# Second mixer of a three-layer kernel: logarithm and exponential for the roots, squares and splits on other engines, rotation and key norms earlier

## The chip, the core and the metric

The kernel runs on one core of a Trainium2 chip. A core has four compute engines that run their own instruction streams and meet through semaphores: TensorE (PE, matrix products; its weight loads are listed as PEld), VectorE (DVE), ScalarE (ACT) and GpSimd (POOL); SyncE (SP) issues most transfers. They share one on-chip memory, SBUF; the products land in eight banks of a second one, PSUM. The metric is the device time of one execution in microseconds (us); lower is better.

## The reference

Three transformer layers run one after the other on 256 tokens (and 256 context tokens) of width 1024, all in float32. The part that matters here is the mixer of the second layer, latent attention with 8 heads. `h` and `hc` are the normalised, modulated tokens and context tokens:

```python
c_q, c_kv, k_pe = split(h @ w_down, [384, 640])      # "down"; widths 384, 256, 64
q = (rmsnorm(c_q, q_lora_norm) @ w_uq)               # "up": 8 heads x (128 + 64), tokens only
kv = (rmsnorm(c_kv, kv_lora_norm) @ w_ukv)           # 8 heads x (128 key + 128 value), tokens and context
q = split_norm(q, q_norm)                            # rmsnorm of the 128 and of the 64 apart
k_nope = rmsnorm(k_nope, k_norm[:128]); k_pe = rmsnorm(k_pe, k_norm[128:])
q[..., 128:], k_pe = rope(q[..., 128:]), rope(k_pe)  # the tokens' own alone
p = softmax(q @ [k_nope, k_pe].T * 192 ** -0.5);  o = p @ v;  x = x + g1 * (o @ w_out)

def rmsnorm(x, g): return x * rsqrt(mean(x * x) + 1e-6) * g
```

## The kernel before

**Weights.** Every weight is streamed once, in slots of 128 x 1024 float32, through a ring of 8 raw buffers that SyncE fills. A product keeps float32 precision by splitting both operands in two: ScalarE copies the raw slot to a rounded `whi` (L369, `hi_slot`, ring of 4), GpSimd subtracts to get `wlo = raw - whi` (L374, `lo_slot`), and TensorE adds the products hi x hi, hi x lo and lo x hi (`slot_products`, L387). The activations are split in the same way. GpSimd does nothing else in this part of the program. The queues are in order on every engine; the order of the work is written out by hand, one function for each engine: `mla_pe`, `mla_act`, `mla_dve`.

**The mixer, on TensorE.** Tokens lie along the columns, features along the partitions. Six "down" tiles come first (`MLA_SRC`): 0 to 2 are the query latents `cq` (256 columns), 3 and 4 the key latents `ckv` (512), 5 the key's rotated part `kpe` (512). Tiles 0 to 3 run paced by the layer's norm; tiles 4 and 5 are whole `column_tile`s. The sum of squares of a latent is a product with a matrix of ones (`down_sums(g)`, L1479; g = 0 query latents, 1 key latents, 2 `kpe`). `mod_turn` transposes a row of the modulation. Then 14 "up" steps follow (`UP`): s = 0 to 5 are two query heads' worth each, 6 to 9 keys, 10 to 13 values. Behind step s = j + 1 stands the sum of the squares of query group j (L1544), which waits for `m_qsq`, the squares themselves; since the queue is in order, step s + 1 stands behind that wait. Behind steps 8 to 11 stand the keys' sums (L1554). Behind step 12 stand three products with a permutation (L1563) that swap the halves for the rotation. `keep_running(pe, 7, 4)` (L460) is four products whose result nobody reads. Products of the modulation (L514) follow, then the scores of the first pair of heads (L1573, L1576).

**On ScalarE.** It evicts each tile from PSUM (L1464 down, L1664 query, L1670 key, L1673 value), squares (L1652 latents, L1668 query), makes `whi`, and takes the roots: for latents a square root (`std`, L627), for queries and keys a logarithm behind each sum (L632) and later, for all together, an exponential (L636, `inverse_root`). When the function set that is loaded lacks the next function, the compiler puts an `ACT_TABLE_LOAD` ahead of it; `preload_act_table_set(LN_EXP)` loads a set with both logarithm and exponential.

**On VectorE.** For latents it takes the reciprocal of the root (L1733), scales (L1738), rounds to the hi part (L1743) and subtracts for the lo part (L1744), which signals `m_clo`; the first up step waits for three of these. Then it squares the keys (L1755), scales the queries (L1748), rotates query and key (L1776 to L1781), and scales the keys (L1760), before the maxima of the scores (L1790).

Of the kernel before, what the change touches and what calls it, by code (L numbers as in the profile page):

```python
# [161 lines left out]
def build(nc, wstream, params, consts, x_in, ctx_in, mem_in, pos_in, w2_in, gla_c, mla_c, sec_c, out):  # L162
    with ExitStack() as ctx:
# [1310 lines left out]
        def mla_pe(pe):  # L1474
# [6 lines left out]
            for m, (name, j, ntok) in enumerate(MLA_SRC):  # L1481
# [16 lines left out]
                elif m >= 4:  # L1498
                    column_tile(pe, START["cq"] + m, DOWN_BANK[m], xhi, xlo, ntok)
                    if m == 4:  # L1500
                        down_sums(0)
                        mod_turn(pe, 5)
            down_sums(1)
            for s, (n, half) in enumerate(UP):
                bank = 2 * (s % 2)
                if s == 0:
                    pe.wait_ge(S["m_clo"], 3)
                    pe.wait_ge(S["m_dn"], 6)
                elif s == 1:
# [26 lines left out]
                if 1 <= s <= 6:  # L1536
# [19 lines left out]
                if s == 12:  # L1556

                    pe.wait_ge(S["m_qn"], 6)
                    pe.wait_ge(S["m_cn"], 6)
                    pe.wait_ge(S["m_klog"], 4)  # L1560
                    pe.wait_ge(S["late_in"], 16)
                    for j, x in enumerate((mq[:, 8:10, :], mq[:, 10:12, :], kpe[:, T:TT])):
                        nc.tensor.matmul(ps[:, 4 + j, 0:T if j == 2 else TT], mlac[:, 0:P], x, start=True, stop=True).then_inc(S["m_sw"], 1)  # L1563
# [76 lines left out]
        def mla_act(act):  # L1640
            def down_std(g):
                m0, cnt, bank, n, ntok = MLA_NORM[g]
                act.wait_ge(S["m_css"], g + 1)
                std(mrst[:, g, 0:ntok], ps[:, bank, 0:ntok], n).then_inc(S["m_cstd"], 1)
            for m, (name, j, ntok) in enumerate(MLA_SRC):
# [7 lines left out]
                if m >= 1:  # L1653
# [3 lines left out]
                if m == 3:  # L1657
                    down_std(0)
            down_std(1)
            for s, (n, half) in enumerate(UP):  # L1660
                up_done(act, s)
                b = 2 * (s % 2)
                if s < 6:
                    nc.scalar.activation(mq[:, 2 * s:2 * s + 2, :], ps[:, b:b + 2, 0:T], ACT.Copy).then_inc(S["m_ev"], 1)  # L1664
                    if s in (0, 3):
                        act.wait_ge(S["m_css"], s // 3 * 2 + 1)
                    act.wait_ge(S["m_ev"], s + 1)
                    nc.scalar.activation(Hf1[:, s, :], mq[:, 2 * s:2 * s + 2, :], ACT.Square).then_inc(S["m_qsq"], 1)  # L1668
# [24 lines left out]
                if s == 11:  # L1693
                    act.wait_ge(S["m_klog"], 4)
                    for i in range(4):
                        inverse_root(Hf1[:, 2 * i:2 * i + 2, :]).then_inc(S["m_krstd"], 1)
# [30 lines left out]
        def mla_dve(dve):  # L1727
# [970 lines left out]
```

## Time and profile before

| | us |
|---|---|
| median of 3 runs | 1294.65 (1293.46 to 1294.67) |
| the profiled execution, whole | 1295.5 |
| its span, first to last instruction | 1293.3 |
| PE busy | 1260.4 (97%) |
| ACT busy | 716.6 (55%) |
| POOL busy | 715.4 (55%) |
| DVE busy | 587.7 (45%) |

The profile lists for each engine the time in which it was busy. The chain that ended last is, at each step, what released the instruction that stood there; in the table of the page 73% of it is PE. The trace lists each instruction with its start, counted from the start of the span. A releaser behind "idle before" is the instruction that ended a wait. Matmuls overlap, so the length of a group of them is some 0.2 us more than the distance to the next group; distances between starts are the safer number. The granted clock is the share of full speed that TensorE was given: 1.00 is 2.4 GHz, 0.5 is 1.2 GHz.

### The profile page before, as it was taken

Reading aid. Unit: us, or ns where it says so; the run is one execution under the profiler, and the core shown is the slowest. Engines: PE = TensorE matmul, PEld = TensorE weight load, DVE = VectorE, ACT = ScalarE, POOL = GpSimd, SP = SyncE. Lnnn points to the kernel's source line nnn. Section 1 sums busy time; section 2 is a strip of 40 time slices with the busy share of each in tenths; the row PEclk is TensorE's granted clock in tenths of the full one; section 3 lists DMA queues with packets and bytes.
Section 4 is the critical chain, followed back from the end, with each engine's and each line's share of the span. In section 5 each row is a group of like instructions: output and inputs, shape, how many; then the busy total and the mean of one; then the engine's idle time right before and its main releaser. Section 6 shows DMA issues by size and latency. Waiting matters only on the chain.

```text
span 1293.3 us, 21900 instructions
## 1 busy us (share of the span) xinstructions
PE 1260.4 (97%) x8008; PEld 1083.7 (84%) x8008; DVE 587.7 (45%) x1065; ACT 716.6 (55%) x1096; POOL 715.4 (55%) x335
## 2 busy tenths in 40 slices
PE   5999999999999999999998999999999999999999
PEld 1688678778888888888777658899999977999999
DVE  3424672237444444210166464555532585666610
ACT  3572356337544544421367554777775667877752
POOL 0442234253444444454445034688898874988897
PEclk8999999999999999999998999999999999999999
DMA  9533753742323333634523334566666540666663
GB/s 362 194 100 106 277 197 131 291 162 73 107 97 97 103 108 97 233 113 135 213 82 116 125 134 161 192 196 195 195 212 197 181 144 33 219 200 193 198 202 129
DMA packets 60132, 210.16 MB, mean 163 GB/s; under 512 B 6432, under 2 KB 9760, under 8 KB 59936
## 3 DMA queue, kind: packets, MB, share of 16 engines
q1 hardware_dynamic: 59632, 207.52, 47.9%
q10 hardware_dynamic: 432, 1.70, 0.3%
q8 instruction: 46, 0.75, 0.2%
q14 instruction: 22, 0.18, 0.0%
HBM read 208.15 MB, written 1.05 MB: 162 GB/s over the span
## 4 chain that ended last, share of the span: by engine, by line
PE 73%; POOL 12%; issue 6%; DVE 4%; ACT 2%; DMA 2%; SPq 0%; POOLq 0%; DVEq 0%; ACTq 0%
PE ps L387 56%; POOL wlo L374 12%; PE ps L514 2%; DMA raw<-wstream 2%; PE ps L1594 1%; PE ps L1573 1%; PE ps L1189 1%; PE ps L442 1%; PE ps L1177 1%; PE ps L424 1%; PE ps L434 1%; ACT whi L369 1%; PE ps L1157 1%; DVE Hlo_ L733 1%; DVE ps L747 1%
## 5 line engine op out<-in xcount | busy, mean ns | idle before, releaser
L374 POOL TENSOR_TENSOR wlo<-raw,whi 128x1024 fp32r<-128x1024 f32 x291 | 687.4, 2381 | 503.7 <-ACT whi L369 503.3
L369 ACT ACTIVATE whi<-raw 128x1024 fp32r<-128x1024 f32 x291 | 306.5, 1057 | 192.9 <-PE ps L387 132.9
L387 PE MATMUL ps<-Hhi_,whi 128*128 128x256 f32 (+1 forms) x1336 | 379.8, 314 | 0.1
L387 PE MATMUL ps<-Hlo_,whi 128*128 128x256 f32 (+1 forms) x1336 | 376.2, 311 | 0.0
L387 PEld LDWEIGHTS ps<-Hhi_,whi 128*128 128x128 f32 x1336 | 255.1, 191 | 16.6 <-issue 4.1
L387 PEld LDWEIGHTS ps<-Hlo_,whi 128*128 128x128 f32 x1336 | 255.1, 191 | 13.6 <-issue 1.4
L387 PE MATMUL ps<-Hhi_,wlo 128*128 128x256 f32 (+1 forms) x1336 | 224.8, 311 | 0.1
L387 PEld LDWEIGHTS ps<-Hhi_,wlo 128*128 128x128 f32 x1336 | 193.8, 191 | 12.7 <-POOL wlo L374 0.3
L387 PE MATMUL ps<-hidhi,whi 128*128 128x256 f32 (+1 forms) x528 | 148.3, 311 | 0.1
L387 PE MATMUL ps<-hidlo,whi 128*128 128x256 f32 (+1 forms) x528 | 147.8, 310 | 0.0
L814 ACT ACTIVATE u<-ps,par 128x256 f32<-128x256 f32 (+1 forms) x132 | 82.6, 626 | 82.5 <-PE ps L387 78.2
L865 DVE SCALAR_TENSOR_TENSOR u<-ps,par,u 128x255 f32<-128x255 f32 (+1 forms) x132 | 73.4, 556 | 81.9 <-ACT u L814 81.9
L387 PEld LDWEIGHTS ps<-hidhi,whi 128*128 128x128 f32 x528 | 100.8, 191 | 6.6 <-DVE XT L989 1.7
L387 PEld LDWEIGHTS ps<-hidlo,whi 128*128 128x128 f32 x528 | 100.8, 191 | 4.7
L989 DVE SCALAR_TENSOR_TENSOR XT<-ps,ada,XT 128x256 f32<-128x256 f32 x48 | 21.6, 479 | 156.1 <-PE ps L387 153.5
L387 PE MATMUL ps<-hidhi,wlo 128*128 128x256 f32 (+1 forms) x528 | 89.1, 310 | 0.0
L868 DVE SCALAR_TENSOR_TENSOR u<-ps,par,u 128x255 f32<-128x255 f32 (+1 forms) x132 | 75.5, 572 | 17.8 <-DVE u L865 0.5
L387 PEld LDWEIGHTS ps<-hidhi,wlo 128*128 128x128 f32 x528 | 76.4, 191 | 4.7
L823 ACT ACTIVATE hidhi<-ps 128x256 f32 (+3 forms) x66 | 52.0, 788 | 45.3 <-DVE ps L876 45.3
L882 DVE TENSOR_TENSOR hidlo<-ps,hidhi 128x256 f32 (+3 forms) x66 | 52.6, 797 | 51.2 <-ACT hidhi L823 51.2
L514 PE MATMUL ps<-raw,cs 128*32 128x512 f32 x304 | 45.4, 645 | 13.5 <-DMA raw<-wstream 13.4
L820 ACT ACTIVATE ps<-u 128x256 f32<-128x256 f32 (+1 forms) x66 | 30.3, 460 | 47.9 <-DVE u L868 47.5
(342 smaller groups left out, 1592.3 us busy)
## 6 DMA issues: line engine op xcount, KB each, us to landing
raw<-wstream SPq DMA_DIRECT2D x367, 512.0 KB, 3.5
Haside_lo<-wstream SPq DMA_DIRECT2D x8, 512.0 KB, 6.1
Haside_hi<-wstream SPq DMA_DIRECT2D x8, 512.0 KB, 9.2
Paside<-wstream SPq DMA_DIRECT2D x4, 512.0 KB, 4.7
XT<-x_t SPq DMA_DIRECT2D x1, 1024.0 KB, 10.6
XT<-ctx_t SPq DMA_DIRECT2D x1, 1024.0 KB, 12.6
memx<-mem_t ACTq DMA_DIRECT2D x1, 1024.0 KB, 5.5
out_t<-XT SPq DMA_DIRECT2D x1, 640.0 KB, 6.1
```

The source lines that it names most:

```text
L369: nc.scalar.activation(whi[:, n % RING, :], raw[:, r % RAWS, :], ACT.Copy).then_inc(S["hi_ready"], 1)
L374: nc.gpsimd.tensor_tensor(wlo[:, r, :], raw[:, r, :], whi[:, n % RING, :].bitcast(F32), ALU.subtract).then_inc(S["lo_ready"], 1)
L387: mm = nc.tensor.matmul(o, a, b, start=start, stop=stop)
L424: nc.tensor.matmul(ps[:, bank, 0:ntok], wlo[:, RAW_OF[n + s] % RAWS, k * P:(k + 1) * P], xhi(k), start=False, stop=False)
L514: mm = nc.tensor.matmul(ps[32 * g:32 * g + 32, MOD_BANK[batch], :], cs[:, k, 6 - 2 * v:38 - 2 * v], rows[:, 512 * (k % 2):512 * (k % 2) + ...
L814: nc.scalar.activation(acc[:, j % 4, :], ps[:, j % 4, 0:ntok], ACT.Identity, scale=pdyn(f"cw{f}_1", i * 8 + j), bias=pdyn(f"cb{f}", i * 8 ...
L820: nc.scalar.activation(ps[:, HID_BANK, 0:ntok], acc[:, (2 * q + 1) % 4, :], ACT.Silu).then_inc(S[f"{t}_s"], 1)
L823: nc.scalar.activation(hid_row(hi, ntok, q, i), in_turn(ps[:, HID_BANK, 0:ntok]), ACT.Copy).then_inc(S[f"{t}_hi"], 1)
L865: nc.vector.scalar_tensor_tensor(seg(acc, 1, T), seg(tile, 0, T - 1), pdyn(f"cw{f}_0", i * 8 + j), seg(acc, 1, T), ALU.mult, ALU.add).then ...
L868: nc.vector.scalar_tensor_tensor(seg(acc, 0, T - 1), seg(tile, 1, T), pdyn(f"cw{f}_2", i * 8 + j), seg(acc, 0, T - 1), ALU.mult, ALU.add). ...
L882: nc.vector.tensor_tensor(hid_row(lo, ntok, q, i), in_turn(hf), hid_row(hi, ntok, q, i).bitcast(F32), ALU.subtract).then_inc(S[f"{t}_pair" ...
L989: ins = nc.vector.scalar_tensor_tensor(x, y, ada[L][:, bass.ds(m * 2 + 16 * part_ + h, 1)], x, ALU.mult, ALU.add)
```

## The change

1. **Latents' roots.** `down_std` takes the logarithm and, right behind it, the exponential, in place of the square root; VectorE's reciprocals (L1733) go. The rounding of the three query latents to their hi part moves from VectorE to ScalarE (`m_chi`).
2. **Sums amid the fifth down tile.** TensorE does tile 4's hi products, then `down_sums(0)`, then tile 4's lo products. ScalarE makes the weight slot that it made behind the second square one square later.
3. **Queries.** The exponential stands behind each logarithm, one group at a time. The squares move from ScalarE (L1668) to VectorE (`query_squares`), where they stand among the splits of the key latents and the scalings of the queries.
4. **Keys.** The exponential stands behind each logarithm too, so the scalings `key_norm` can follow one by one; all four stand ahead of the first maxima.
5. **Rotation.** The permutation of `kpe` moves behind step 2, that of the queries behind step 7, and VectorE's rotations with them.
6. **Rest.** Up steps use the other pair of PSUM banks, `keep_running` goes, and `out_act("mo")` no longer loads the set LN_EXP.

```diff
@@ out_act
-            nc.scalar.preload_act_table_set(LN_EXP)
+            if stage != "mo":
+                nc.scalar.preload_act_table_set(LN_EXP)
@@ mla_pe
-                elif m >= 4:
+                elif m == 4:
+                    n = START["cq"] + m
...
+                    for o, c0, width, _, x, start, stop in his:
+                        nc.tensor.matmul(o, whi[:, n % RING, c0:c0 + width], x, start=start, stop=stop)
+                    down_sums(0)
+                    pe.wait_ge(S["lo_ready"], n + 1)
+                    for o, c0, width, _, x, start, stop in los:
+                        mm = nc.tensor.matmul(o, wlo[:, RAW_OF[n] % RAWS, c0:c0 + width], x, start=start, stop=stop)
+                    mm.then_inc(S["slot_used"], 1)
+                    mod_turn(pe, 5)
+                elif m == 5:
                     column_tile(pe, START["cq"] + m, DOWN_BANK[m], xhi, xlo, ntok)
-                    if m == 4:
-                        down_sums(0)
-                        mod_turn(pe, 5)
...
-                bank = 2 * (s % 2)
+                bank = 2 * ((s + 1) % 2)
...
+                    if j == 3:
+                        pe.wait_ge(S["m_rot"], 1)
...
+                if s == 2:
...
+                    nc.tensor.matmul(ps[:, 7, 0:T], mlac[:, 0:P], kpe[:, T:TT], start=True, stop=True).then_inc(S["m_sw"], 1)
+                if s == 7:
+                    pe.wait_ge(S["m_qn"], 6)
+                    for j, x in enumerate((mq[:, 8:10, :], mq[:, 10:12, :])):
+                        nc.tensor.matmul(ps[:, 6 + j, :], mlac[:, 0:P], x, start=True, stop=True).then_inc(S["m_sw"], 1)
...
-            keep_running(pe, 7, 4)
+            pe.wait_ge(S["m_klog"], 4)
@@ mla_act
-                std(mrst[:, g, 0:ntok], ps[:, bank, 0:ntok], n).then_inc(S["m_cstd"], 1)
+                alink(log_square(mrst[:, g, 0:ntok], ps[:, bank, 0:ntok], n))
+                inverse_root(mrst[:, g, 0:ntok]).then_inc(S["m_cstd"], 1)
...
+                    for k in range(3):
+                        act.wait_ge(S["m_cn"], k + 1)
+                        nc.scalar.activation(cqhi(k), in_turn(mla_dst(k)), ACT.Copy).then_inc(S["m_chi"], 1)
...
-                    nc.scalar.activation(Hf1[:, s, :], mq[:, 2 * s:2 * s + 2, :], ACT.Square).then_inc(S["m_qsq"], 1)
...
+                    act.wait_ge(S["m_qlog"], j + 1)
+                    inverse_root(query_root(j)).then_inc(S["m_qrstd"], 1)
@@ mla_dve
-                nc.vector.reciprocal(mrst[:, g, 0:ntok], mrst[:, g, 0:ntok]).then_inc(S["m_crv"], 1)
...
+            def query_squares(j):
...
+                x = mq[:, 2 * j:2 * j + 2, :]
+                nc.vector.tensor_tensor(Hf1[:, j, :].rearrange("p (a t) -> p a t", t=T), x, x, ALU.mult).then_inc(S["m_qsq"], 1)
...
+            for m in range(3):
+                latent_norm(m)
+            for m in range(3):
+                dve.wait_ge(S["m_chi"], m + 1)
+                nc.vector.tensor_tensor(cqlo(m), in_turn(mla_dst(m)), cqhi(m).bitcast(F32), ALU.subtract).then_inc(S["m_clo"], 1)
+            latent_norm(3)
+            key_split(3)
+            query_squares(0)
+            latent_norm(4)
+            key_split(4)
+            latent_norm(5)
+            query_squares(1)
+            query_squares(2)
...
+            for j in range(3, 6):
+                query_squares(j)
+                query_norm(j - 3)
```

The first place is TensorE's queue at the fifth down tile (L387 before, L1504 and L1508 after: its products; L1479, L1480: the sums of the query latents; L533: `mod_turn`). Before:

```order
L387 MATMUL ps<-Hhi_,whi 128x512
L387 MATMUL ps<-Hlo_,whi 128x512
L387 MATMUL ps<-Hhi_,wlo 128x512 [waits lo_ready]
L387 MATMUL ps<-Hhi_,wlo 128x512 x7
L1479 MATMUL ps<-Hf,con 128x256 [waits m_csq]
L1479 MATMUL ps<-Hf,con 128x256 x2
L533 MATMUL ps<-sel,modrow 128x8 [waits mod_row]
```

And now:

```order
L1504 MATMUL ps<-Hhi_,whi 128x512
L1504 MATMUL ps<-Hlo_,whi 128x512
L1480 MATMUL ps<-Hf,con 128x256 [waits m_csq]
L1480 MATMUL ps<-Hf,con 128x256 x2
L1508 MATMUL ps<-Hhi_,wlo 128x512 [waits lo_ready]
L1508 MATMUL ps<-Hhi_,wlo 128x512 x7
L533 MATMUL ps<-sel,modrow 128x8 [waits mod_row]
```

The three sums have moved ahead of the tile's eight lo products.

The second place is VectorE's queue behind the query latents' splits. Before (L1733 reciprocal, L1738 scaling, L1743 rounding, L1744 lo part, L1755 squares of the keys):

```order
L1733 RECIPROCAL mrq<-mrq 128x512 [waits m_cstd]
L1738 SCALAR_TENSOR_TENSOR ckv<-ckv,par,mrq 128x512 [waits m_crv]
L1743 CAST ckvhi<-ckv 128x256x2 [waits m_cn]
L1744 TENSOR_TENSOR ckvlo<-ckv,ckvhi 128x256x2 [waits dve_step]
L1738 SCALAR_TENSOR_TENSOR ckv<-ckv,par,mrq 128x512
...
L1738 SCALAR_TENSOR_TENSOR kpe<-kpe,par,mrq 128x512 [waits m_crv]
L1755 TENSOR_TENSOR Hf<-kn 128x1024 [waits m_qss,m_ev,m_cn]
```

Now (L1751 scaling, L1757 and L1758 the split, L1766 squares of the queries, L1771 their scaling):

```order
L1751 SCALAR_TENSOR_TENSOR ckv<-ckv,par,mrq 128x512 [waits m_cstd]
L1757 CAST ckvhi<-ckv 128x256x2 [waits m_cn]
L1758 TENSOR_TENSOR ckvlo<-ckv,ckvhi 128x256x2 [waits dve_step]
L1766 TENSOR_TENSOR Hf<-mq 128x512 [waits m_css,m_ev]
L1751 SCALAR_TENSOR_TENSOR ckv<-ckv,par,mrq 128x512 [waits m_cstd]
...
L1751 SCALAR_TENSOR_TENSOR kpe<-kpe,par,mrq 128x512 [waits m_cstd]
L1766 TENSOR_TENSOR Hf<-mq 128x512 [waits m_ev] x2
```

The reciprocals are gone, and the squares of the first query group stand right behind the split of the first key latent.

The third place is ScalarE's queue at the first two up steps (L1664 eviction, L1668 squares, L369 `whi`, L627 square root, L632 logarithm). Before:

```order
L1664 ACTIVATE mq<-ps 128x512 [waits slot_used]
L1668 ACTIVATE Hf<-mq 128x512 [waits m_ev]
L369 ACTIVATE whi<-raw 128x1024 [waits slot_used,raw_in0]
L632 ACT_TABLE_LOAD
L632 ACTIVATE mrq<-ps,con 128x512 [waits m_qss]
```

Now (L1684 eviction, L636 exponential):

```order
L1684 ACTIVATE mq<-ps 128x512 [waits slot_used]
L369 ACTIVATE whi<-raw 128x1024 [waits slot_used,raw_in0]
L632 ACTIVATE mrq<-ps,con 128x512 [waits m_qss]
L636 ACTIVATE mrq<-mrq 128x512 [waits m_qlog]
```

The squares and the load are gone, and the exponential is new. No `ACT_TABLE_LOAD` is left between the down projection and the end of the output projection.

## Rows read from the trace of the kernel before

**Rows 1.** TensorE's timeline, 655 to 745 us: start, length, line, [idle before].

```profile
678.05 1.88 PE L1479 MATMUL ps<-Hf,con 128*128 128x512 f32 x4
683.39 2.93 PE L387 MATMUL ps<-cqsplit,whi 128*128 128x256 f32 x12 [3.46 <-DVE cqsplit L1744]
```

**Rows 2.** The chain that ended last, 665 to 760 us: start, length, what.

```profile
683.39 4.21 PE ps L387 x18
687.60 1.71 PE ps L1479 x2
689.31 2.19 PE ps L387 x18
691.50 0.86 PE ps L1544 x2
692.37 2.01 PE ps L387 x18
...
734.43 1.73 PE ps L460 x8
```

**Rows 3.** Busy time by stretches; PEclk is the granted share of the clock.

```profile
core 0: us, PE busy (x) PEld busy (x) DVE busy (x) ACT busy (x) POOL busy (x), PEclk, DMA share, GB/s
...
683.40:691.34 7.94, 7.94 (x38) 6.91 (x39) 7.77 (x7) 2.75 (x4) 1.35 (x1) 0.61 0.22 66
...
739.66:794.60 54.94, 53.79 (x268) 34.46 (x265) 32.27 (x53) 25.86 (x55) 9.93 (x4) 1.00 0.32 120
```

**Rows 4.** VectorE's timeline, 655 to 745 us and 739 to 815 us.

```profile
673.08 0.50 DVE L1730 TENSOR_SCALAR gsc<-par 128x2 f32<-128x2 f32 x1
...
679.38 0.62 DVE L1744 TENSOR_TENSOR cqsplit<-cq,cqsplit 128x256 fp32r<-128x256 f32 x1
...
680.77 2.57 DVE L1744 TENSOR_TENSOR cqsplit<-cq,cqsplit 128x256 fp32r<-128x256 f32 x1
...
686.55 0.75 DVE L1738 SCALAR_TENSOR_TENSOR ckv<-ckv,par,mrq 128x512 f32<-128x512 f32 x1
687.33 0.64 DVE L1743 CAST ckvhi<-ckv 128x512 fp32r<-128x512 f32 x1
688.01 1.10 DVE L1744 TENSOR_TENSOR ckvlo<-ckv,ckvhi 128x512 fp32r<-128x512 f32 x1
...
707.58 1.88 DVE L1755 TENSOR_TENSOR Hf<-kn 128x1024 f32<-128x1024 f32 x1 [10.19 <-ACT kn L1670]
...
714.26 1.22 DVE L1755 TENSOR_TENSOR Hf<-kn 128x1024 f32<-128x1024 f32 x1
...
771.40 2.99 DVE L1799 TENSOR_SCALAR Pm<-Pm,arec 128x512 f32<-128x512 f32 x2
```

**Rows 5.** GpSimd's timeline, 640 to 830 us.

```profile
680.53 2.34 POOL L374 TENSOR_TENSOR wlo<-raw,whi 128x1024 fp32r<-128x1024 f32 x1 [3.34 <-ACT whi L369]
...
706.02 2.36 POOL L374 TENSOR_TENSOR wlo<-raw,whi 128x1024 fp32r<-128x1024 f32 x1 [0.30 <-ACT whi L369]
...
771.50 2.62 POOL L374 TENSOR_TENSOR wlo<-raw,whi 128x1024 fp32r<-128x1024 f32 x1 [1.58 <-ACT whi L369]
```

**Rows 6.** ScalarE's timeline, 655 to 745 us.

```profile
678.25 0.60 ACT L1464 ACTIVATE kpe<-ps 128x512 f32<-128x512 f32 x1 [3.50 <-PE ps L387]
...
679.42 1.04 ACT L369 ACTIVATE whi<-raw 128x1024 fp32r<-128x1024 f32 x1
680.36 0.67 ACT L627 ACTIVATE mrq<-ps,con 128x512 f32<-128x512 f32 x1
...
687.64 0.60 ACT L1664 ACTIVATE mq<-ps 128x512 f32<-128x512 f32 x1 [6.61 <-PE ps L387]
...
711.63 0.61 ACT L636 ACTIVATE cq<-cq 128x512 f32<-128x512 f32 x1
```

**Rows 7.** ScalarE's function-set loads in groups by line, 657 to 740 us.

```profile
L632 ACT ACT_TABLE_LOAD x2 | 2.6, 1283 | 0.0
L636 ACT ACT_TABLE_LOAD x2 | 2.6, 1283 | 0.0
...
L627 ACT ACT_TABLE_LOAD x1 | 1.3, 1283 | 0.0
```

**Rows 8.** DMA issues of weight slots, whole run: count, size, median us to landing.

```profile
raw<-wstream SPq DMA_DIRECT2D x367, 512.0 KB, 3.5
```

More of the change, by code:

```diff
@@ L1550, in mla_pe @@
                         pe.wait_ge(S["m_qlog"], 6)
+                    if i == 1:
+                        pe.wait_ge(S["m_rot"], 2)
                     if i >= 2:
@@ L1555, in mla_pe @@
                     mm.then_inc(S["m_kss"], 1)
[L1556 to L1563, printed above, removed]
             def scores(p, qt):
@@ L1692, in mla_act @@
                     log_square(Hf1[:, 2 * i:2 * i + 2, :], ps[:, 4 + 2 * (i % 2):6 + 2 * (i % 2), :], 128).then_inc(S["m_klog"], 1)
[L1693 to L1696, printed above, removed]
+                    act.wait_ge(S["m_klog"], i + 1)
+                    inverse_root(Hf1[:, 2 * i:2 * i + 2, :]).then_inc(S["m_krstd"], 1)
             def exps(p, qt):
@@ new lines, in mla_dve @@
+            latent_norm(5)
+            query_squares(1)
+            query_squares(2)
+            dve.wait_ge(S["m_sw"], 1)
+            dlink(nc.vector.tensor_tensor(Hf1[:, 7, 0:T], ps[:, 7, 0:T], sin, ALU.mult))
+            dve.wait_ge(S["m_cn"], 6)
+            dlink(nc.vector.tensor_tensor(kpe[:, T:TT], kpe[:, T:TT], cos, ALU.mult))
+            nc.vector.tensor_tensor(kpe[:, T:TT], kpe[:, T:TT], Hf1[:, 7, 0:T], ALU.add).then_inc(S["m_rot"], 1)
+            for j in range(3, 6):
+                query_squares(j)
+                query_norm(j - 3)
@@ L1761, in mla_dve @@
+            query_norm(3)
             key_squares(0)
-            dve.wait_ge(S["m_qrstd"], 1)
-            for j in range(3):
-                query_norm(j)
+            query_norm(4)
+            query_norm(5)
             key_squares(1)
-            for j in range(3, 6):
-                query_norm(j)
-            key_squares(2)
-            key_squares(3)
             dve.wait_ge(S["m_qn"], 6)
             dve.wait_ge(S["m_sw"], 3)
-            dve.wait_ge(S["late_in"], 16)
-            cos, sin = mlac[:, P:P + T], mlac[:, P + T:P + 2 * T]
@@ L1777, in mla_dve @@
             dlink(nc.vector.tensor_tensor(x, x, cos.rearrange("p (a t) -> p a t", a=1).to_broadcast([P, 4, T]), ALU.mult))
+            key_squares(2)
+            dve.wait_ge(S["m_rot"], 2)
             nc.vector.tensor_tensor(x, x, tmp, ALU.add).then_inc(S["m_rot"], 1)
-            dlink(nc.vector.tensor_tensor(mrst[:, 0, 0:T], ps[:, 6, 0:T], sin, ALU.mult))
-            dlink(nc.vector.tensor_tensor(kpe[:, T:TT], kpe[:, T:TT], cos, ALU.mult))
-            nc.vector.tensor_tensor(kpe[:, T:TT], kpe[:, T:TT], mrst[:, 0, 0:T], ALU.add).then_inc(S["m_rot"], 1)
@@ L1783, in mla_dve @@
             key_norm(0)
-            key_norm(1)
+            key_squares(3)
+            for i in range(1, 4):
+                key_norm(i)
             def maxes(p, qt):
```

58 lines of the change are left out of this document (29 added, 29 removed).

## The prediction

> **What bounds the kernel now.** I read the busy table first: PE is busy 97% of the span, so the change can only help by removing TensorE work, a TensorE wait, or time at the lower clock. The edits lie in the second mixer, so I read TensorE's timeline there. It has one long wait: the second latents' sums start at 678.05 and the first up step at 683.39, 3.46 us idle, released by VectorE's last lo part of the query latents [rows 1]. Behind it the granted clock of the next 7.94 us is 0.61, a mix of 1.2 and 2.4 GHz, though TensorE is busy throughout [rows 3]. In the chain that ended last the same work shows it: an up step of 18 products takes 4.21 and then 2.19 us, where the third takes 2.01; the sum between them takes 1.71, where a later one takes 0.86 [rows 2]. So one late split costs 3.46 us idle and (1 - 0.61) x 7.94 = 3.1 us of slow clock. Third, `keep_running` holds TensorE for 1.73 us [rows 2], 1.8 with its hand-over. From the first scores to the second output tile TensorE is busy 53.79 of 54.94 us [rows 3], so nothing that VectorE or ScalarE do sooner there is worth more than a microsecond.
>
> **Part 1 and 2, latents' roots and the sums amid tile 4.** The sums come ahead of eight lo products, and their root has no table load ahead of it. ScalarE can then have the inverse root by about 671.4. VectorE is held until its modulation bias and `gsc`, 673.08 + 0.50 [rows 4], since these stand ahead and wait for `mod_turn`, whose place on TensorE does not move. From 673.6 it has three scalings and three lo parts (0.5 and 0.6 us each, the latter [rows 4]), with ScalarE's rounding beside them: done at about 676.5 to 677, against 679.8 when TensorE wants them. The split is no longer late, by a margin of 3 us; even a GpSimd piece of 2.4 us in between keeps it. The 3.46 us and the 3.1 us go: **-6.6**. TensorE's own products stay the same in number. The reciprocals that go were hidden for keys and `kpe`, and the added exponentials (0.6 us each by the 512-column one, [rows 6]) lie on a ScalarE that waits for TensorE.
>
> **Part 6.** `keep_running` goes: -1.8. The four products of modulation unit 9 read raw slots, and the last of these is freed only when the last up step ends; a slot lands a median 3.5 us after its issue [rows 8], and TensorE now wants it some 3.1 us later (seven of the eight slots' products at 0.45 us). I take a wait of 0.2, between 0 and 0.6: **-1.6**.
>
> **Table loads.** Five of 1.28 us go inside the mixer [rows 7] and one more in the output projection. ScalarE waits for TensorE around them all, except that the first lay in the latents' root, counted above. Worth nothing more: 0.
>
> **Part 3, the squares on VectorE.** This is the step that decides. First what the rows show. A VectorE instruction with both inputs in SBUF waits when GpSimd is in a piece of `wlo`. The lo part that takes 0.62 us alone took 2.57 when it started at 680.77, with a GpSimd piece from 680.53 to 682.87; it ended 0.47 after the piece. The squares of the keys take 1.22 us alone, and 1.88 when started at 707.58 inside the piece of 706.02 to 708.38 [rows 4, 5]. And the port changes hands between two VectorE instructions when GpSimd asks: two scalings started at 771.40 took 2.99 together, because a piece asked at 771.50, waited 0.27 (2.62 for 2.35) and then ran between them [rows 4, 5]. Before the change the query squares were on ScalarE, which the rows never show waiting so.
>
> The Trainium skill states the same in "SBUF — State Buffer", section Who interferes with whom: a VectorE instruction with two SBUF inputs and a GpSimd instruction that reads SBUF exclude each other for the whole instruction, and whichever issued first keeps the port. The rows agree (2.57 for 0.62). By a reading of the edit without this rule the total below would be 7 us lower; it speaks against this part of the change.
>
> Now the schedule after. TensorE: sums end 679.8; step 0 2.0, the `kpe` sum 0.86, step 1 2.0 [rows 2]: at 684.7 it wants the squares of query group 0, which VectorE must have made. ScalarE: `kpe` is evicted at 678.25, the slot copy at 679.42 ends at 680.46 and the root at 680.36 moves behind it as now [rows 6], logarithm 0.67 and exponential 0.6: the keys' root is there at 681.6. GpSimd starts its piece at 680.53, as before [rows 5]. VectorE therefore asks for the first key latent's scaling at 681.65, inside the piece; it runs at 682.75 and ends at 683.5 (0.75). The rounding takes 0.64, to 684.2. By then ScalarE has evicted step 0 (681.8 + 0.2 drain, 0.60) and copied the next slot (1.04, to 683.5), so GpSimd is in its next piece, 683.6 to 685.95. The lo part of 1.10 us waits for it and ends at 686.9. During it the slot copy behind step 1's eviction ends (684.9 + 0.5 + 1.04 = 686.4), GpSimd asks and takes the port at 686.8, as at 771.50, to 689.1. The squares of group 0 are next on VectorE: they wait for this third piece and end at 689.7 (0.69 us, an estimate between half the 1.22 of the keys' squares and the 0.75 of a scaling of the same size). TensorE waits from 684.7 to 689.75: **+5.1**. Everything behind it on TensorE, steps 2 to 13, waits along.
>
> The clock: a wait of 3.46 us was followed by 3.1 us lost, so one of 5.1 will be too. Bounds 0 (the clock does not fall) and 3.4 (a little more than the one case); I take **+2.8**, since VectorE is the slower of the two in part of that stretch.
>
> Groups 1 to 5: the path from a step's end to its squares is eviction 0.6, a wait of up to 2.3 for a piece, 0.7, against the 2.0 + 0.86 us of TensorE's next step and sum. Group 1 stands behind the second key split and `kpe`, and is wanted about when it is ready (0 to 0.7 late). Of groups 3 to 5, one or two will start within a piece, one of them behind a scaling that did too: 1.5 to 2.1 late. I take **+1.8**, bounds 0 and 5 x 0.8.
>
> **Parts 4 and 5.** Rotation and key scalings all have VectorE time: behind step 7 it has no GpSimd piece beside it, since the last slot ahead of the output projection is made behind step 5. ScalarE's logarithm and exponential of 1.1 us each per key step fit in TensorE's 4.3. The scores wait for the modulation products as before: 0, at most 0.3. The three added waits on TensorE (`m_rot` ahead of sum 3 and of the second keys' sum, `m_qn` behind step 7) hold the later up steps; the last may show 0.3, inside the bounds above.
>
> **Sum.** -6.6 - 1.6 + 5.1 + 2.8 + 1.8 = +1.5, I round the interaction of the late terms down to +1.3. The profiled execution took 1295.5 (span 1293.3 and 2.2 around it), 0.85 above the median of the runs; measured against that median, 1294.65 + 1.3 = 1296.0. A measurement of this kernel tells 0.2% (2.6 us) from no change.
>
> **The rivals.**
> - *The port costs little here.* If squares and splits ran beside GpSimd, group 0's would be ready by 684.8, and the waits left are 1.1 us in all: -6.6 - 1.8 + 1.1 = -7.3, 1287.3. The 2.57 and 1.88 us rows speak against it, but they are a handful of cases. 0.15.
> - *A milder stall.* VectorE keeps the port when its squares stand right behind the lo part (the wait at TensorE is then 2.9, not 5.1), or the clock does not fall: 1.3 - 2.2 or 1.3 - 2.8, so 1292.5 to 1294. 0.17.
> - *Slower: every group queues behind a piece.* The price is eviction 0.65 + 2.25 + 0.7 = 3.6 per step where TensorE gives 2.9 minus the sum's start, 2.0: up to 1.6 late for each of groups 1 to 5. It decides when GpSimd's copy-ready slots keep arriving between a step's eviction and its squares, which is where ScalarE puts them (the slot copy stands right behind the eviction). Three groups more than forecast: +1.3 + 3.3 and up, 1298.5 to 1301. 0.13.
>
> **How the numbers follow.** Forecast 0.55, around 1296.0, from 1294.5 to 1298. The range leaves out the first rival (0.15) and the far end of the last (0.05): 1291.0 to 1299.5. Faster than 1292.06: 0.15 + 0.04 of the milder stall = 0.19. Slower than 1297.2: 0.13 + 0.05 of the forecast's upper end = 0.18. Within: 0.63.
>
> **What would show it.** In the profile after: no idle time ahead of step 0 and full clock there; instead an idle time of 4 to 5.5 us on TensorE ahead of the sum of query group 0, released by VectorE's squares at L1766, and about 0.6 granted clock behind it; VectorE's lo part L1758 and squares L1766 at over 2 us where they take 1.1 and 0.7 alone, with GpSimd pieces that end just before they do. The prediction is wrong if L1766 stays at 0.7 us beside running pieces, or if TensorE's wait there is under 1 us. The scores should start at 740 to 741.5 where they started at 739.66 of the span.

## The result and the profile after

The changed kernel takes 1300.39 us (median of 6 runs, 1299.35 to 1301.05) beside 1294.62 us for the kernel before on the same chip (6 runs, 1293.46 to 1296.77): 1.004 times the time, 95% interval 1.003 to 1.0049. On another chip it was 1299.78 beside 1295.78 us, 1.003 (1.0019 to 1.0042). It is slower, by 4.0 to 5.8 us; the forecast was 1296.0, no change to be measured, and the range ended at 1299.5.

The page of after shows the same busy shares as before, but PE is busy 2 us less in a span 4.7 us longer, so TensorE waits more.

```profile
span 1298.0 us, 21885 instructions
PE 1258.5 (97%) x8000; PEld 1082.0 (83%) x8000; DVE 590.4 (45%) x1065; ACT 710.9 (55%) x1094; POOL 717.0 (55%) x335
```

TensorE's timeline of after, where [rows 1] stood (start, length, [idle before]), then its weight loads:

```profile
680.75 1.90 PE L387 MATMUL ps<-cqsplit,whi 128*128 128x256 f32 x12
...
691.31 2.08 PE L1556 MATMUL ps<-Hf,con 128*128 128x512 f32 x2 [5.12 <-DVE Hf L1766]
692.40 3.55 PE L387 MATMUL ps<-cqsplit,whi 128*128 128x256 f32 x12
...
708.07 1.13 PE L1556 MATMUL ps<-Hf,con 128*128 128x512 f32 x2 [1.95 <-DVE Hf L1766]
...
715.49 1.98 PE L1564 MATMUL ps<-mq,mlac 128*128 128x512 f32 x4 [0.25 <-DVE mq L1771]
...
739.81 4.61 PE L514 MATMUL ps<-raw,cs 128*32 128x512 f32 x32
```

```profile
743.36 0.14 PEld L514 LDWEIGHTS ps<-raw,cs 128*32 128x32 f32 x4 [0.83 <-DMA raw<-wstream]
```

The first up step (680.75) no longer waits, and it runs at full speed. In its place stand 5.12 us ahead of the first sum of squares, 1.95 and 0.25 us behind, and a DMA wait inside the modulation products, which take 4.61 us. Before they took 3.64:

```profile
736.09 3.64 PE L514 MATMUL ps<-raw,cs 128*32 128x512 f32 x32
```

VectorE and GpSimd at the long wait, where [rows 4, 5] stood:

```profile
683.11 1.72 DVE L1751 SCALAR_TENSOR_TENSOR ckv<-ckv,par,mrq 128x512 f32<-128x512 f32 x1 [5.02 <-ACT mrq L636]
684.87 0.73 DVE L1757 CAST ckvhi<-ckv 128x512 fp32r<-128x512 f32 x1
685.64 2.98 DVE L1758 TENSOR_TENSOR ckvlo<-ckv,ckvhi 128x512 fp32r<-128x512 f32 x1
688.48 2.78 DVE L1766 TENSOR_TENSOR Hf<-mq 128x512 f32<-128x512 f32 x1
...
694.22 0.67 DVE L1766 TENSOR_TENSOR Hf<-mq 128x512 f32<-128x512 f32 x1
```

```profile
679.55 4.74 POOL L374 TENSOR_TENSOR wlo<-raw,whi 128x1024 fp32r<-128x1024 f32 x2 [4.30 <-ACT whi L369]
684.99 2.68 POOL L374 TENSOR_TENSOR wlo<-raw,whi 128x1024 fp32r<-128x1024 f32 x1 [0.70 <-ACT whi L369]
687.85 2.86 POOL L374 TENSOR_TENSOR wlo<-raw,whi 128x1024 fp32r<-128x1024 f32 x1 [0.18 <-ACT whi L369]
```

The square that takes 0.67 us alone takes 2.78 when it starts at 688.48 inside GpSimd's piece of 687.85 to 690.71; it ends 0.55 behind it. The granted clock behind the wait, where [rows 3] stood, is 1.2 GHz (0.50), though TensorE is busy throughout. From the scores on, TensorE needs the same 54.94 us as in [rows 3]:

```profile
691.31:696.80 5.49, 5.49 (x19) 4.46 (x20) 3.51 (x5) 1.32 (x2) 0.00 (x0) 0.50 0.00 0
...
744.34:799.28 54.94, 53.79 (x266) 34.51 (x265) 29.97 (x51) 24.52 (x54) 9.94 (x4) 1.00 0.31 118
```

**The measure used below.** The change acts between the first product of the fourth down tile (number 3) and the first score. I call this stretch R. Behind its end every trace has 553.6 to 553.7 us of its span left. R is 82.40 us in the trace of before and 85.71 in that of after: +3.3, where the forecast's sum was +1.3. The first score starts at 744.34, where 740 to 741.5 was forecast: 1.4 of this lies ahead of R, 3.3 in it. What lies ahead of R is the same work in all kernels, yet R begins at 657.26 to 660.53 us in the fourteen traces. So R is the measure of the change in a trace. The profiled executions in which R begins latest (e6, e7, e8 below) took 1.9 to 3.5 us more than the medians of their kernels.

### The profile page after: what moved, and what is told of

Its sections match the earlier page's. It is cut to its first block, busy times and chain, and to the rows that moved or that the text cites. A ratio compares the mean times of both kernels' runs of the same rounds, so it can differ in the third digit from the quotient of the medians.

```text
span 1298.0 us, 21885 instructions
## 1 busy us (share of the span) xinstructions
PE 1258.5 (97%) x8000; PEld 1082.0 (83%) x8000; DVE 590.4 (45%) x1065; ACT 710.9 (55%) x1094; POOL 717.0 (55%) x335
## 4 chain that ended last, share of the span: by engine, by line
PE 72%; POOL 12%; issue 6%; DVE 5%; ACT 3%; DMA 2%; SPq 1%; POOLq 0%; DVEq 0%; ACTq 0%
PE ps L387 55%; POOL wlo L374 12%; PE ps L514 2%; DMA raw<-wstream 2%; PE ps L1608 1%; PE ps L1587 1%; PE ps L1190 1%; PE ps L442 1%; PE ps L1178 1%; SPq L347 1%; PE ps L424 1%; PE ps L434 1%; ACT whi L369 1%; PE ps L1158 1%; DVE Hlo_ L733 1%
## 5 line engine op out<-in xcount | busy, mean ns | idle before, releaser
L369 ACT ACTIVATE whi<-raw 128x1024 fp32r<-128x1024 f32 x291 | 306.6, 1057 | 195.1 <-PE ps L387 134.2
L387 PE MATMUL ps<-Hhi_,whi 128*128 128x256 f32 (+1 forms) x1328 | 376.8, 313 | 0.1
L387 PE MATMUL ps<-Hlo_,whi 128*128 128x256 f32 (+1 forms) x1328 | 373.2, 311 | 0.0
L387 PEld LDWEIGHTS ps<-Hhi_,whi 128*128 128x128 f32 x1328 | 253.6, 191 | 16.3 <-issue 4.1
L387 PEld LDWEIGHTS ps<-Hlo_,whi 128*128 128x128 f32 x1328 | 253.6, 191 | 13.4 <-issue 1.4
L387 PE MATMUL ps<-Hhi_,wlo 128*128 128x256 f32 (+1 forms) x1328 | 223.0, 311 | 0.1
L387 PEld LDWEIGHTS ps<-Hhi_,wlo 128*128 128x128 f32 x1328 | 192.3, 191 | 12.5 <-POOL wlo L374 0.3
L387 PE MATMUL ps<-hidhi,whi 128*128 128x256 f32 (+1 forms) x528 | 148.3, 311 | 0.1
L387 PE MATMUL ps<-hidlo,whi 128*128 128x256 f32 (+1 forms) x528 | 147.8, 310 | 0.0
L814 ACT ACTIVATE u<-ps,par 128x256 f32<-128x256 f32 (+1 forms) x132 | 82.7, 626 | 82.4 <-PE ps L387 78.0
L387 PEld LDWEIGHTS ps<-hidhi,whi 128*128 128x128 f32 x528 | 100.8, 191 | 6.7 <-DVE XT L989 1.7
L387 PEld LDWEIGHTS ps<-hidlo,whi 128*128 128x128 f32 x528 | 100.8, 191 | 4.7
L387 PE MATMUL ps<-hidhi,wlo 128*128 128x256 f32 (+1 forms) x528 | 89.1, 310 | 0.0
L387 PEld LDWEIGHTS ps<-hidhi,wlo 128*128 128x128 f32 x528 | 76.4, 191 | 4.7
```

Of the source, the lines that this page charges most:

```text
L369: nc.scalar.activation(whi[:, n % RING, :], raw[:, r % RAWS, :], ACT.Copy).then_inc(S["hi_ready"], 1)
L387: mm = nc.tensor.matmul(o, a, b, start=start, stop=stop)
L814: nc.scalar.activation(acc[:, j % 4, :], ps[:, j % 4, 0:ntok], ACT.Identity, scale=pdyn(f"cw{f}_1", i * 8 + j), bias=pdyn(f"cb{f}", i * 8 ...
```

## The experiments

Ten more kernels ran, and both kernels once more, each beside the kernel before on its own chip (medians of before 1294.76 to 1295.78 us). R and the waits are those of the one profiled execution of each; "DMA" is the wait inside the modulation products. "Theory P" is the prediction's: a VectorE instruction with two SBUF inputs waits for GpSimd's piece.

| kernel | median us | ratio (95%) | R us | waits of TensorE in R, us |
|---|---|---|---|---|
| before, first and second trace | | | 82.40, 81.12 | 3.46 |
| after, first and second trace | | | 85.71, 86.18 | 5.1, 1.95, 0.25, DMA |
| e1_latents | 1289.94 | 0.996 (0.9947-0.9974) | 75.72 | none |
| e8_latents_nokeep | 1288.34 | 0.9947 (0.9934-0.996) | 75.18 | DMA |
| e7_latents_squares | 1296.99 | 1.0014 (1.0005-1.0023) | 84.03 | 5.08 |
| e2_psum | 1295.4 | 1.0002 (0.9993-1.0011) | 81.20 | 2.96, 2.00, 0.40, DMA |
| e3_act | 1299.56 | 1.003 (1.0018-1.0043) | 85.01 | 6.05, 1.25, DMA |
| e5_act_late | 1292.05 | 0.9979 (0.997-0.9988) | 77.86 | 0.20, 1.63, DMA |
| e4_fill | 1297.09 | 1.0013 (1.0004-1.0021) | 83.05 | 1.19, 0.54, 1.23, DMA |
| e6_keep | 1299.85 | 1.0038 (1.0026-1.005) | 85.79 | 5.09, 1.94, 0.25 |
| e9_short_all | 1290.64 | 0.9968 (0.9956-0.998) | 77.02 | 0.26, 0.63, 0.25, DMA |
| e10_short_first | 1296.89 | 1.0022 (1.0012-1.0032) | 86.75 | 2.23, 4.75, 1.22, DMA |

**1. Parts 1 and 2 alone (e1).** The kernel before with the new latents' roots, the split on ScalarE and the sums amid tile 4:

```diff
-                std(mrst[:, g, 0:ntok], ps[:, bank, 0:ntok], n).then_inc(S["m_cstd"], 1)
+                alink(log_square(mrst[:, g, 0:ntok], ps[:, bank, 0:ntok], n))
+                inverse_root(mrst[:, g, 0:ntok]).then_inc(S["m_cstd"], 1)
...
+                    down_sums(0)
+                    pe.wait_ge(S["lo_ready"], n + 1)
```

> The kernel before with the change's parts 1 and 2 alone: logarithm and exponential for the latents' roots, ScalarE's rounding of the query latents, the sums amid the fifth down tile. Query squares stay on ScalarE, the rotation, the key norms and keep_running stay where they were. Theory P (VectorE and GpSimd exclude each other when VectorE reads two SBUF inputs, and that hits the moved squares and the moved permutation): nothing here makes TensorE wait for such an instruction, so the 3.46 us wait and the 3.1 us at the lower clock go and nothing comes back: 1288 us, 6 to 7 below before; granted clock 1.00 throughout the mixer. Rival Q (the late keys' root or the sums amid tile 4 are what costs, not the squares): the first up steps wait here too, by 3 us or more, and the time is 1292 or more.

R falls by 6.68 us; no wait is left, and the clock stays at 1.00. That is the forecast's -6.6; by the medians it is 5.6 (3.4 to 6.9). GpSimd's pieces (685.90 to 694.40) hold VectorE up there too:

```profile
686.70 2.83 DVE L1753 SCALAR_TENSOR_TENSOR ckv<-ckv,par,mrq 128x512 f32<-128x512 f32 x1
689.56 2.75 DVE L1759 CAST ckvhi<-ckv 128x512 fp32r<-128x512 f32 x1
692.34 3.04 DVE L1760 TENSOR_TENSOR ckvlo<-ckv,ckvhi 128x512 fp32r<-128x512 f32 x1
```

```profile
685.90 3.08 POOL L374 TENSOR_TENSOR wlo<-raw,whi 128x1024 fp32r<-128x1024 f32 x1 [1.44 <-ACT whi L369]
689.22 5.18 POOL L374 TENSOR_TENSOR wlo<-raw,whi 128x1024 fp32r<-128x1024 f32 x2 [0.24 <-ACT whi L369]
```

This costs nothing, since TensorE wants the key latents only at step 6. Note the CAST: 2.75 us, with one SBUF input.

**2. The squares on top (e7).** e1 with part 3's squares on VectorE, the first behind the first key split:

```diff
+            latent_norm(3)
+            key_split(3)
+            query_squares(0)
```

> The run with the latents' parts alone (e1_latents), plus the move of the query squares to VectorE, in the place that the change gives them (the first behind the split of the first key latent, the others behind the kpe scaling). Theory P: the wait of 5.1 us ahead of the first query sum comes back, with 1.7 to 3.4 us at the lower clock behind it, and nothing else: 7 to 8.5 us above e1_latents, about 1297. Rival Q (it needs the rest of the change too): below 3 us above e1_latents.

```profile
690.35 2.78 DVE L1769 TENSOR_TENSOR Hf<-mq 128x512 f32<-128x512 f32 x1
```

```profile
693.18 2.08 PE L1553 MATMUL ps<-Hf,con 128*128 128x512 f32 x2 [5.08 <-DVE Hf L1769]
```

R rises by 8.3 us, to 84.03: one wait of 5.08 us, and 1.2 GHz behind it. By the medians it is 7 us. This one move eats all that parts 1 and 2 give.

**3. One operand of the square from PSUM (e2).** After, with the step's PSUM bank in place of one `mq`:

```diff
-                nc.vector.tensor_tensor(Hf1[:, j, :].rearrange("p (a t) -> p a t", t=T), x, x, ALU.mult).then_inc(S["m_qsq"], 1)
+                nc.vector.tensor_tensor(Hf1[:, j, :].rearrange("p (a t) -> p a t", t=T), ps[:, b:b + 2, 0:T], x, ALU.mult).then_inc(S["m_qsq"], 1)
```

> The changed kernel with one edit: the query squares read one of their two operands from PSUM instead of the SBUF copy. Engine, order and waits are the same. Theory P: the squares no longer wait for GpSimd; they stay at about 0.7 us beside a running piece. The lo part ahead of them still waits (2.6 to 3 us). TensorE's wait ahead of the first query sum falls from 5.1 to about 2.9, ahead of the second one it is 0.7 to 2.4, the one ahead of the fifth sum (1.95) goes; the clock may hold. 3 to 5 us below the changed kernel, 1295.5 to 1297.5. Rival R (the squares are late because VectorE has too much in its queue, whatever it reads): no difference beyond 0.5 us, and the squares still take over 2 us.

```profile
684.83 2.99 DVE L1758 TENSOR_TENSOR ckvlo<-ckv,ckvhi 128x512 fp32r<-128x512 f32 x1
687.68 0.66 DVE L1767 TENSOR_TENSOR Hf<-ps,mq 128x512 f32<-128x512 f32 x1
```

GpSimd's piece beside the square is there as in after:

```profile
687.09 2.83 POOL L374 TENSOR_TENSOR wlo<-raw,whi 128x1024 fp32r<-128x1024 f32 x1 [0.22 <-ACT whi L369]
```

The lo part ahead is as slow as in after (2.99), but the square takes 0.66 where it took 2.78: with the same work and the same place, the second SBUF operand costs 2.1 us. The wait falls by 2.2, and the clock doesn't fall. The median, 1295.4, lies 0.1 below the range expected.

**4. The squares back on ScalarE (e3), and with the key's rotation late (e5).** After, without VectorE's squares:

```diff
+                    nc.scalar.activation(Hf1[:, s, :], mq[:, 2 * s:2 * s + 2, :], ACT.Square).then_inc(S["m_qsq"], 1)
...
-            query_squares(0)
```

> The changed kernel with the query squares back on ScalarE behind each eviction, as before the change; all else as changed. Theory P: the wait ahead of the first sum goes, but the permutation of kpe stands behind step 2 on TensorE and needs VectorE's kpe scaling, which stands behind two key splits that each wait for a GpSimd piece. The wait moves there: 5 to 6 us ahead of L1564's kpe product, slow clock behind it, and the time stays within 1 us of the changed kernel, 1299.5 to 1301.5. Rival S (the move of the squares is the whole loss): 7 to 9 us below the changed kernel, 1291.5 to 1293.5.

As expected, this was no gain (R 85.01): part 5's rotation is a second customer of the same queue.

```profile
695.97 1.22 PE L1560 MATMUL ps<-kpe,mlac 128*128 128x256 f32 x2 [6.05 <-DVE kpe L1755]
```

```profile
686.58 2.83 DVE L1755 SCALAR_TENSOR_TENSOR ckv<-ckv,par,mrq 128x512 f32<-128x512 f32 x1
689.45 2.70 DVE L1761 CAST ckvhi<-ckv 128x512 fp32r<-128x512 f32 x1
692.18 1.09 DVE L1762 TENSOR_TENSOR ckvlo<-ckv,ckvhi 128x512 fp32r<-128x512 f32 x1
693.13 2.79 DVE L1755 SCALAR_TENSOR_TENSOR kpe<-kpe,par,mrq 128x512 f32<-128x512 f32 x1
```

TensorE reaches the permutation behind step 2 sooner, while GpSimd's pieces hold up the scalings ahead of `kpe`. In e5 the permutation stands behind step 7 as well:

```diff
-                if s == 2:
+                if s == 7:
```

> As the run with the squares back on ScalarE, and the permutation and rotation of kpe beside those of the queries, behind step 7. Theory P: no TensorE wait over 2 us is left ahead of step 8, at most 1 to 2 us ahead of the query permutation; no slow clock. 7.5 us below the changed kernel, about 1293; 1291.5 to 1294.5. Rival: if early kpe was not the second obstacle, this equals the run before it.

R is 77.86: both early customers of VectorE have to go, then the gain of parts 1 and 2 shows.

**5. TensorE kept busy in the wait (e4).** After, with 9 products (18 in the trace) that nobody reads ahead of the first sum:

```diff
+                    if j == 0:
+                        keep_running(pe, 7, 9)
```

> The changed kernel with nine products whose result nobody reads (9 x 0.43 = 3.9 us, keep_running in a free PSUM bank) ahead of TensorE's wait for the first query squares. They fill the wait of 5.1 us, so nothing is delayed. Theory P: the remaining wait is 1.2 us, the clock stays at 1.00, and the 2.75 us lost behind the wait come back, less what later squares then miss (up to 1): 1.7 to 2.8 below the changed kernel, 1297.6 to 1298.7. If the slow clock cost nothing, the time is the changed kernel's, 1300.4.

```profile
685.48 4.05 PE L460 MATMUL ps<-con 128*128 128x256 f32 x18
690.73 1.13 PE L1558 MATMUL ps<-Hf,con 128*128 128x512 f32 x2 [1.19 <-DVE Hf L1768]
```

TensorE gets the squares as late as without the filler, but the clock stays at 2.4 GHz, and R is 2.66 us shorter. Nearly all of that is the price of the clock; the later waits moved as well (0.54 and 1.23 us, where after has 1.95 and 0.25), which is 0.4 us of idle time less.

**6. `keep_running` back (e6), and taken from e1 (e8).**

```diff
+            keep_running(pe, 7, 4)
```

> The changed kernel with keep_running put back ahead of the modulation products. If the transfer of unit 9's last slot is what TensorE waits for there (0.97 us), the four products of 1.83 us hide it, and the time rises by 0.9 us, 0.4 to 1.4 above the changed kernel, and TensorE shows no wait for the DMA in L514. If the wait had another cause, it rises by 1.8.

> e1_latents without keep_running. Its four products took 1.83 us of TensorE, but unit 9's last raw slot is freed only when the last up step ends; the changed kernel lost 0.97 us there. So 0.9 us below e1_latents, 0.4 to 1.4; if the slot's transfer were in time, 1.8 below. TensorE should show a wait of about 0.5 us for the DMA in L514.

TensorE in e6:

```profile
740.50 1.89 PE L460 MATMUL ps<-con 128*128 128x256 f32 x8
742.33 3.64 PE L514 MATMUL ps<-raw,cs 128*32 128x512 f32 x32
```

The modulation products take 3.64 us behind it, as before, and 4.61 in after without it; in e8 the first score starts 4.76 us after their start, where it was 3.57. So the removal of 1.8 gives back 1.0 to 1.2. In e8 0.54 us is left. In e6 I expected 0.4 to 1.4 us more than in after, and R is only 0.08 above after's: TensorE worked at 1.2 GHz only from 692.76 to 696.90, and 2.07 us were lost, where after lost 2.75. Without that difference it is 0.8. The medians don't tell so little apart (e6 1.0038, after 1.004 and 1.003).

**7. GpSimd's pieces shortened (e9, e10).** After, with pieces of 64 instead of 1,024 columns (the line of e9, which shortens all ten slots of the up steps; e10 shortens the second to the fourth alone). The products with these low parts read the high parts instead (not shown), so TensorE's work stays and the result is not the reference's:

```diff
+            w = 64 if n in range(START["uq"], START["mo"]) else 8 * P
+            nc.gpsimd.tensor_tensor(wlo[:, r, 0:w], raw[:, r, 0:w], whi[:, n % RING, 0:w].bitcast(F32), ALU.subtract).then_inc(S["lo_ready"], 1)
```

> The changed kernel, in which GpSimd works out the low parts of the ten slots of the mixer's up-projections over 64 columns instead of 1,024; the products with those low parts read the high parts instead, so that TensorE's work and all waits stay as they are (the result of these projections is not that of the reference). Theory (GpSimd's piece keeps VectorE's instruction with two operands in SBUF waiting): in the trace the part lo of the fourth latent tile, the first square, the rotation of the key and the later squares take 0.65 to 1.2 us instead of 2.5 to 3.0 us, the wait of 5.1 us ahead of the first sum of squares falls below 1 us, that of 1.95 us below 0.5 us, and the clock doesn't fall: the stretch from the third tile's first product to the first score is 75 to 78 us instead of 85.7 and 86.2 us (85.95 - 5.1 - 2.2 - 1.95 = 76.7, and up to 1 us of waits left), the ratio 0.9955 to 0.9975. Rival (VectorE is slow there by its own operands or by its order of work, and GpSimd's piece only lies beside it): the durations stay at 2.5 to 3.0 us, the wait at 4 to 5 us, the stretch at 84 to 86 us, the ratio at 1.002 to 1.004. Rival (the slow square is GpSimd's, but the wait comes mainly from the order of the latents ahead of the squares): short durations, but a wait of 2 us or more, and 80 us or more.

```profile
682.41 0.75 DVE L1752 SCALAR_TENSOR_TENSOR ckv<-ckv,par,mrq 128x512 f32<-128x512 f32 x1 [5.65 <-ACT mrq L637]
683.20 0.72 DVE L1758 CAST ckvhi<-ckv 128x512 fp32r<-128x512 f32 x1
683.96 1.13 DVE L1759 TENSOR_TENSOR ckvlo<-ckv,ckvhi 128x512 fp32r<-128x512 f32 x1
684.93 0.77 DVE L1767 TENSOR_TENSOR Hf<-mq 128x512 f32<-128x512 f32 x1
```

Same queue, same operands, no long piece beside them: nothing is slow, the waits are 0.26 and 0.63, and R is 77.02, inside the 75 to 78 expected. With the same work in the same order on VectorE and no long pieces the stall is gone, so GpSimd's pieces are the cause.

> As the kernel with all ten slots shortened, but for the second to the fourth slot of the query up-projection alone: the pieces that lie beside the latents and the first square, from 682 to 691 us of the trace of after. Theory (two separate prices, the first wait with the fall of the clock behind it, and the later waits): the first wait falls from 5.1 us below 1 us and the clock stays at full speed, while the wait ahead of the fifth sum (1.95 us) stays between 1 and 2.5 us: the stretch is 77 to 80.5 us (85.95 - 5.1 - 2.2 = 78.7), the ratio 0.9965 to 0.9995, and the difference to the kernel with all ten shortened, 1 to 3 us, is what the later groups cost. Rival (what the first square gains comes back at the later groups, because the later pieces then meet other squares): the later waits grow to 4 us or more in sum, and the stretch is above 81 us.

Here I missed. GpSimd works further ahead of TensorE than I had counted: the three short pieces stood at about 672, 678 and 681 us, ahead of the latents, and the full ones began in time to meet the first square:

```profile
684.36 5.60 POOL L375 TENSOR_TENSOR wlo<-raw,whi 128x1024 fp32r<-128x1024 f32 x2 [2.74 <-ACT whi L369]
```

```profile
687.81 1.12 PE L1557 MATMUL ps<-Hf,con 128*128 128x512 f32 x2 [2.23 <-DVE Hf L1767]
695.70 2.08 PE L1557 MATMUL ps<-Hf,con 128*128 128x512 f32 x2 [4.75 <-DVE Hf L1767]
```

In this execution the first wait fell to 2.23, the next grew to 4.75, with 1.2 GHz behind it, and R rose to 86.75. The stall moved with the phase of the pieces. But this is one of the three slowest of eleven runs (1299.98 to 1300.86; the other eight took 1295.27 to 1298.35). The median is 2.1 us above before, where after is 4.0 to 5.8 above; it misses the 0.9965 to 0.9995 expected too. What the waits are in the usual execution of e10 is not shown.

**8. Both kernels again (b2, a2).**

> The kernel before, profiled a second time, nothing changed. Theory (part of the change's cost seen in the first pair of traces is not its own): in the first trace of before the first layer's output projection ended at 249.74 us, in the traces of the other kernels, whose instructions up to there are the same, at 249.8 to 252.6 us, because a weight slot lands 0.1 to 3 us later. Then this second trace shows that point at 250 to 252.5 us, a span 0.5 to 2.5 us above the first one's 1293.3 us, and the same 82.4 us (within 0.3 us) between the third tile's first product and the first score. Rival (the early point belongs to the kernel before): the point is again at 249.7 to 249.8 us and the span at 1293 us. Timed ratio against itself 1.000, within 0.001.

> The changed kernel, profiled a second time beside the kernel before. The region between the third tile's first product and the first score was 85.7 us in its first trace and 82.4 us in that of before. Theory (the region is all that the change does): 85.7 us again within 0.4 us, with one wait of some 5.1 us ahead of the first sum of squares and the clock at half speed for 6.8 us behind it, and a timed ratio of 1.0026 (+3.3 us, 1.0015 to 1.0035), below the 1.0044 of the first pair, because there 1.4 us came from a weight slot far ahead of the change. Rival (the change costs something outside that region too): a ratio of 1.004 or more on this chip as well, and an earlier point in the first layer that is again later than that of before on the same chip by 1 us or more.

Medians 1295.48 and 1299.78 us, ratios 0.9998 (0.9988 to 1.0007) and 1.003 (1.0019 to 1.0042). In the first trace of before a weight slot of the first layer landed earlier than in that of after; the second trace of before has it late as well. ScalarE's copy of that slot in before, then in its second trace:

```profile
238.55 1.06 ACT L369 ACTIVATE whi<-raw 128x1024 fp32r<-128x1024 f32 x1 [10.62 <-DMA raw<-wstream]
```

```profile
239.85 1.06 ACT L369 ACTIVATE whi<-raw 128x1024 fp32r<-128x1024 f32 x1 [11.26 <-DMA raw<-wstream]
```

So that difference isn't the change's. But the span of the second trace is 1293.3 us all the same, and R 81.12: my expectations of a longer span and of 82.4 missed. Its step 0 shows where the 1.3 us came back (TensorE; [rows 1] has 683.39 and 2.93):

```profile
684.66 1.67 PE L387 MATMUL ps<-cqsplit,whi 128*128 128x256 f32 x12 [3.46 <-DVE cqsplit L1744]
686.13 1.49 PE L387 MATMUL ps<-cqsplit,wlo 128*128 128x256 f32 x6
```

The same wait of 3.46 us, but 1.2 GHz began only at 686.1, behind the wait, where in the first trace it began at 682.7, within it; full speed was back at about the same time, 689.5. The clock's loss was 1.7 us instead of 3.1. The second trace of after has R 86.18, 0.1 above the range that I expected, and TensorE's time at 1.2 GHz stands in two stretches there (to 693.5, and from 707.2 to 710.6), not in one.

## Why the prediction was wrong, point by point

- **Parts 1 and 2, -6.6: right in mechanism.** e1 measured -6.7 against the first trace of before, but -5.4 against the second, and -5.6 by the medians.
- **Part 3, +5.1: right in mechanism, place and size.** 5.12 and 5.07 us in the two traces of after, and the three pieces came within 0.4 us of the schedule, the later start of R taken off. e7 shows the move does it, e2 that the second SBUF operand does (2.1 us of it), e9 that GpSimd's pieces do.
- **The clock, +2.8: right, the size partly by luck.** (696.80 - 691.31) / 2 = 2.75 in after; e4, without it, is 2.66 shorter. But the reason given for less than 3.1, a slower VectorE, has no row behind it. What counts is how much of the stretch at 1.2 GHz TensorE works through, and behind the same 5.1 us wait that cost 2.07 us in e6, 3.1 in e7 and 3.2, in two stretches, in the second trace of after.
- **First failed step: part 6, -1.6.** It held that the DMA wait takes 0.2 back, 0 to 0.6 at most. It takes 1.0 (4.61 for 3.64), in e8 1.2; the gain is 0.5 to 0.9. The 3.5 us from issue to landing [rows 8] were right. TensorE waits for the one slot that is issued at 739.91, when the last up step has freed it (the transfers' line L347 of after, 738 to 740.3 us):

```profile
DMA to landing us min/median/max: 3.4/3.4/3.4
```

Wrong was the time at which TensorE wants it. I counted seven slots' products, 3.1 us. But the weight loads run ahead of the products: before, the last slot's load starts 2.60 us behind the first one (736.09 to 738.69), in after 3.56 (739.80 to 743.36), and that is the 0.96 us. In e8 the slot took 3.6 and the load came at 3.78. And even 3.5 - 3.1 is 0.4, not the 0.2 that I took.
- **Second failed step: the later groups, +1.8, too small.** 1.95 and 0.25 us are idle in the records, about 2.5 with the hand-overs; -6.7 - 0.8 + 5.1 + 2.75 leaves some 3 for them of the +3.3 of R. My bounds (0 to 4) held it, and the pattern was as forecast, one late group of 1.5 to 2.1.
- **Rounding down** +1.5 to +1.3 had no row behind it.
- **A number by the way.** The forecast says that the total would be 7 us lower without the port rule. By its own first rival, 1287.3, it is 8.7.
- **From R to the median.** The error in R is 2.0 us: mainly 1.2 of the later groups, 0.8 of part 6 and 0.2 of the rounding. By itself it would leave 1298.0, inside the range. The measured differences of the medians, 4.0 and 5.8, are above the 3.3 of the first pair of traces, and this takes the time out of the range. The mean of R over both traces of each kernel differs by 4.2 (85.95 - 81.76). My range took the one trace of before as exact, while its 3.1 us at the slow clock is 1.7 in another execution: parts 1 and 2 could only give back what was there. With that in the bounds, -5.2 instead of -6.6, the sum's upper end is 1.4 higher.
- **The rivals.** "The port costs little" is refuted (e9, e2). The median lies in the span of the slower rival, 1298.5 to 1301, but its mechanism isn't what happened: only one later group waits long (1.95), where it wanted three more. That VectorE keeps the port for squares right behind the lo part was refuted too: the piece at 687.85 went in between.

Two things are not settled. What decides when 1.2 GHz begins, within a wait or behind it, was not tested. And 1.6 us of the first chip's difference (5.8 beside the 4.2 of R) have no place in the account; the second chip's 4.0 agrees with R, and the two intervals overlap, so I claim no cause.

**The better version.** The change's parts 1 and 2 without `keep_running` (e8) take 1288.34 us, 0.9947 of before: the lowest median of all that ran, though its interval overlaps with that of e1. It keeps GpSimd's full pieces, which e9 (1290.64) leaves out: nothing that TensorE wants soon stands behind VectorE's slow instructions.

## What to carry to other kernels

Before a small operation moves to VectorE, list its SBUF operands and what GpSimd does at that time: beside back-to-back GpSimd pieces of 2.4 us, a 0.7 us square cost 2.8, and a short queue of them became a 5 us wait. When a transfer can only start once its buffer is freed, count from there to the weight load that wants it, not to the product: the loads ran 0.5 us ahead here. And where a stretch at the slow clock is part of the gain, look at it in a second trace before counting it in full.

## What the runs showed of the hardware that was not expected

- **A conversion with one SBUF input waits for GpSimd too.** The CAST from f32 to fp32r of 128x512 took 2.75 us (e1) and 2.70 us (e3) beside a piece, 0.64 to 0.73 alone. The forecast had it free. The Trainium skill's "SBUF — State Buffer", Who interferes with whom, lists cast among the operations that can enter a mode with both ports, under conditions on the operands, and so contend with GpSimd; these rows agree.
- **The same wait costs the clock different amounts.** 3.46 us of waiting went with a loss of 3.1 us in one execution of the kernel before and 1.7 us in the other; 5.1 us of waiting with 2.75, 2.07 (e6), 3.1 (e7) and, with a second fall, 3.2 us; 6.05 us (e3) with 2.2. Mostly 1.2 GHz began within the wait, 0.4 (second trace of after) to 2.7 us (e6) ahead of its end, and what passed of it while TensorE stood idle cost nothing; in the second trace of before it began 1.4 us behind the wait's end. Behind 2.96 us (e2) the clock did not fall; behind 1.95 us it did in the second trace of after, at about 707.2 us, and not in the first, nor behind 2.23 us in e10.
